# Decoder step on one core: another order of the work in the paged sample attention, and one barrier instead of two at each stage's end

## What is computed

```python
z = rms_norm(h, g) @ w_in
o_a = sparse attention, 8 query heads on 2 K/V heads, top 256 keys of an indexer
o_b = softmax over three dilated windows' denominators, of their outputs
h += (sigmoid(g_A) * (o_a @ w_br_a) + sigmoid(g_B) * (o_b @ w_br_b)) @ w_out
h += memory attention(rms_norm(h)) ; h += swiglu(rms_norm(h)) ; y = rms_norm(h)
```

```python
s = jnp.einsum('bqhgd,bqkhd->bqhgk', qg, k_sel).astype(jnp.float32) * ATTN_SCALE
s = jnp.where(valid[:, :, None, None, :], s, -jnp.inf)
p = jax.nn.softmax(s, axis=-1)
o = jnp.einsum('bqhgk,bqkhd->bqhgd', p.astype(v_sel.dtype), v_sel)
```

```python
wts = jax.nn.softmax(jnp.stack(lses, axis=0), axis=0)
o = jnp.einsum('gbth,gbthd->bthd', wts, jnp.stack(outs, axis=0).astype(jnp.float32))
```

## Time and profile before

| what | value |
|---|---|
| median of three runs | 2143.05 us (2139.27 to 2144.12) |
| profiled execution | 2131.45 us |
| its span | 2129.6 us |
| PE busy | 1971.6 us (93%) |
| DVE busy | 1292.5 us (61%) |
| ACT busy | 709.7 us (33%) |
| POOL busy | 617.9 us (29%) |

### The profile page before, as it was taken

One profiled execution on the slowest core, in us unless ns is written; L12 is line 12 of the kernel. 1 busy time (PEld: TensorE's weight loads), 2 busy tenths in 40 slices (PEclk: granted clock), 3 DMA queues, 4 the chain that ended last, 5 costly groups with the idle time before them and its releaser, 6 DMA issues. The chain is left out here.

```text
span 2129.6 us, 35124 instructions
## 1 busy us (share of the span) xinstructions
PE 1971.6 (93%) x13501; PEld 1815.2 (85%) x13501; DVE 1292.5 (61%) x2478; ACT 709.7 (33%) x1456; POOL 617.9 (29%) x720
## 2 busy tenths in 40 slices
PE   6999899999999896899589989899999999999997
PEld 6878798999997794555379988899999999999997
DVE  5049999999970454543456234786676766643535
ACT  5243222112212572343222135643232332332423
POOL 5786647678980232100200110300000000301000
PEclk9999999999999896999889999899999999999999
DMA  5022232345855726871366102022222222635334
GB/s 178 19 85 76 67 91 78 105 152 176 257 167 159 246 64 170 278 257 60 102 190 177 40 22 80 25 63 81 81 71 86 73 84 81 217 96 166 128 91 137
DMA packets 224858, 254.16 MB, mean 119 GB/s; under 512 B 51684, under 2 KB 206468, under 8 KB 224180
## 3 DMA queue, kind: packets, MB, share of 16 engines
q1 hardware_dynamic: 192292, 170.92, 26.9%
q0 software_dynamic: 9360, 54.37, 7.2%
q10 hardware_dynamic: 23040, 26.63, 3.5%
HBM read 205.18 MB, written 74.00 MB: 131 GB/s over the span
## 5 line engine op out<-in xcount | busy, mean ns | idle before, releaser
L955 PE MATMUL pz<-w_hi,n_hi 128*128 128x384 f32 (+2 forms) x720 | 245.3, 341 | 0.6 <-issue 0.5
L955 PE MATMUL pz<-w_hi,n_lo 128*128 128x384 f32 (+2 forms) x720 | 239.3, 332 | 0.0
L955 PE MATMUL pz<-w_lo,n_hi 128*128 128x384 f32 (+2 forms) x720 | 239.2, 332 | 0.0
L862 DVE MATCH_REPLACE8 sel<-m,sel 128x1024 f32<-128x1024 f32 (+4 forms) x224 | 205.6, 923 | 0.0
L859 DVE MAX8 m<-sel 128x8 f32<-128x1024 f32 (+4 forms) x224 | 197.8, 927 | 0.2
L3618 PE MATMUL p_c<-n_t_hi,blk 128*128 128x264 f32 x1120 | 191.3, 285 | 1.8 <-DVE blk L3335 1.8
L3618 PEld LDWEIGHTS p_c<-n_t_hi,blk 128*128 128x128 f32 x1120 | 159.0, 188 | 2.0 <-issue 2.0
L955 PEld LDWEIGHTS pz<-w_hi,n_hi 128*128 128x128 f32 x720 | 137.6, 191 | 17.0 <-issue 14.9
L3618 PE MATMUL p_c<-mix_hi,blk 128*128 128x264 f32 x816 | 141.1, 285 | 0.0
L955 PEld LDWEIGHTS pz<-w_hi,n_lo 128*128 128x128 f32 x720 | 137.7, 191 | 0.0
L955 PEld LDWEIGHTS pz<-w_lo,n_hi 128*128 128x128 f32 x720 | 137.7, 191 | 0.0
(11 more groups left out here) (490 smaller groups left out, 5194.9 us busy)
## 6 DMA issues: line engine op xcount, KB each, us to landing
w_raw<-in_w_in SPq DMA_DIRECT2D x26, 768.0 KB, 4.6
blk_raw<-in_w_ffn_in SPq DMA_DIRECT2D x72, 256.0 KB, 2.9
relu<-z_qb SPq DMA_DIRECT2D x24, 512.0 KB, 4.9
blk_raw<-in_w_ffn_out SPq DMA_DIRECT2D x58, 192.0 KB, 2.5
z_b<-z ACTq DMA_DIRECT2D x48, 192.0 KB, 1.9
gates<-z ACTq DMA_DIRECT2D x48, 176.0 KB, 3.0
gate<-gates SPq DMA_DIRECT2D x24, 352.0 KB, 3.6
out_new_win_sample<-in_cache_win_kv POOLq DMA_DIRECT2D x8, 1016.0 KB
```

What stands on the lines that cost most here:

```text
L862: dve.match_replace(out=sel[0:r, o:o + n], in_to_replace=m8[0:r, u, :], in_values=sel[0:r, o:o + n], imm_value=PICKED).then_inc(s_rep, 1)
L955: m = pe.matmul(out, tokens(a, k, i), b[:, n % 2, k, 0:w], start=(k == 0 and p == 0), stop=(k == KC - 1 and p == 2))
```

## The change

It has two parts.

**One barrier.** The callback at a stage's end no longer has the second barrier. POOL still clears the semaphores behind the Block's own barrier; the freed numbers are put at the end of the list of free ones, so that the next stage takes others. Seven stages have it.

**Order in `attend_sample_a`.** PE turns the keys of b = 6 right behind those of 5, and lays the bias and the scores of 4 and 5 and the keys of 7 ahead of the first half's turned probabilities, and the scores of 6 and 7 behind them; `values` is split in `turn_probs` and `values`. Row tiles 0 and 1 stand before `values(0)`, tiles 2 to 7 behind `values(1)`. DVE does the first half's differences, shares and weighted sum before it looks at the second half's weights; then `soft(0)` and `soft(1)`, two row tiles, `out(0)`, `out(1)`, six row tiles. ACT's second exponential for the shares moves behind the keys of b = 5; the exponential of a softmax (`exps`) is split from the copies. No operation is added or removed in the stage.

```diff
-    ctx.callback(lambda: (nc.clear_and_free_semaphores(handles), nc.all_engine_barrier()))
+    def retire():
+        nc.clear_and_free_semaphores(handles)
+        nums = [h.num for h in handles]
+        nc.reset_free_semaphores([x for x in nc.free_semaphores if x not in nums] + nums)
+
+    ctx.callback(retire)
...
+                for b in range(6):
+                    keys(b)
+                    if b in (1, 5):
+                        shares(b // 5)
+                keys(6)
+                exps(0)
+                keys(7)
+                weights(0)
+                for i in range(BETWEEN):
+                    rest_high(i)
+                exps(1)
+                weights(1)
+                for i in range(BETWEEN, NT):
...
-                nearest(0)
-                nearest(1)
                 shares(0)
-                shares(1)
                 dve.wait_ge(s_share, 1)
...
+                shares(1)
...
+                soft(0)
+                soft(1)
+                for i in range(BETWEEN):
+                    rest_low(i)
+                out(0)
+                out(1)
+                for i in range(BETWEEN, NT):
...
-                    if i >= BETWEEN:
-                        pe.wait_ge(s_ptev, 3 if i < 2 * BETWEEN else 6)
+                    pe.wait_ge(s_ptev, 3 if i < BETWEEN else 6)
...
-                def values(u):
+                def turn_probs(u):
+                    pe.wait_ge(s_exp, u + 1)
                     for c in range(3):
-                        pe.wait_ge(s_exp, u + 1)
-                        if c == 0:
-                            pe.wait_ge(s_chi, BETWEEN * (u + 1))
-                            pe.wait_ge(s_clo, BETWEEN * (u + 1))
+                        if u and c == 0:
+                            pe.wait_ge(s_chi, BETWEEN)
+                            pe.wait_ge(s_clo, BETWEEN)
...
+                for b in (0, 2, 4):
+                    if b % 4 == 0:
+                        bias_and_new(b // 4)
+                    if b < 4:
+                        for c in range(2):
+                            turn_half(b + 2, c)
+                    for c in range(2):
+                        score_pair(b, c)
+                    for c in range(2):
+                        turn_half(b + 3, c)
+                    if b == 2:
+                        for c in range(2):
+                            turn_half(6, c)
+                turn_probs(0)
+                for c in range(2):
+                    score_pair(6, c)
+                for i in range(BETWEEN):
+                    turn_rows(i)
+                values(0)
+                turn_probs(1)
+                values(1)
+                for i in range(BETWEEN, NT):
```

More of the change, by code:

```diff
@@ L1953, in weights @@
                 def weights(u):
-                    act.wait_ge(s_sm, u + 1)
-                    act.activation(probs[:, 0:NKS], probs[:, 0:NKS], ACT.Exp, scale=-1.0, bias=st[:, u, 0:1],
-                                   accum_out=st[:, u, 1:2]).then_inc(s_exp, 1)
                     for c in range(3):
@@ L1966, in shares, with exps @@
                     act.activation(ex[:, :, x, :], ex[:, :, x, :], ACT.Exp).then_inc(s_ex, 1)
[L1968 to L1976, removed]
+                def exps(u):
+                    act.wait_ge(s_sm, u + 1)
+                    act.activation(probs[:, 0:NKS], probs[:, 0:NKS], ACT.Exp, scale=-1.0, bias=st[:, u, 0:1],
+                                   accum_out=st[:, u, 1:2]).then_inc(s_exp, 1)
+                for b in range(6):
[11 more added lines that the diff above has]
+                for i in range(BETWEEN, NT):
                     rest_high(i)
@@ L2008, in _, with shares @@
                 q.then_inc(s_qexp, 1)
-                def nearest(half):
+                def shares(half):
                     x = slice(HALF * half, HALF * (half + 1))
@@ L2018, in nearest @@
                     t.then_inc(s_diff, 1)
-                def shares(half):
-                    x = slice(HALF * half, HALF * (half + 1))
                     dve.wait_ge(s_ex, half + 1)
@@ L2142, in values @@
                         t.then_inc(s_pt, 1)
+                def values(u):
                     pe.wait_ge(s_ptev, 3 * u + 3)
```

## The result

| what | before | changed |
|---|---|---|
| median of five runs | 2141.34 us (2139.27 to 2144.12) | 2122.64 us (2118.13 to 2130.16) |
| span of the profiled execution | 2129.6 us | 2120.8 us |
| sample attention, release to release | 64.0 us | 50.7 us |

The ratio is 0.9916, with a 95% interval of 0.9898 to 0.9934: between 14 and 22 us less, 18.0 in the middle. The forecast was 19.6 less (2123.5, the measured median is 2122.64). The ratio with its interval is what is used from here on; quotients of the medians differ from it by up to about 0.001. The ratios are of executions at one speed: one execution of the kernel with 26 transposes, at 2419.11 us and a mean granted clock of 0.755, is in none of them.

What follows compares the result with a forecast made beforehand. PE bounds most stages, standing still longest in `attend_sample_a`, where it waited 11.35 us for DVE's late sum. Stage 15.4 plus barriers 4.2 make 19.6 us off the median 2143.05: 2123.5 us, range 2117 to 2131.

Steps and rivals of the forecast that it cites:

- `values(0)`: First half's values on PE in the sample attention: 3.9 us, from 1047.84 to 1051.73 in the earlier trace.
- `values(1)`: Second half's values on PE in the sample attention: 4.0 us, from 1066.46 to 1070.46 in the earlier trace.
- DVE's chain: DVE up to the first softmax in the sample attention: weighted sum alone, 7.4 us instead of 13.45; `soft(0)` done at 1034.65.
- the new wait: PE waits for `s_sm` at the second bias, after turning keys 5 and 6; about 5 us, released by DVE's L2047.
- The bound of 13.45: Upper bound in us on DVE's weighted sum if nothing becomes faster; as a rival, 2129.5 us in total, chance 0.09.
- the block behind the new wait: PE's bias, scores of 4 and 5 and keys 7, within a term of 7.95 us that also held later scores and row tiles.
- a rival on `merge`: PE's clock stays low through 228 more records in `merge`: 30 us lost, 2153.5 us; chance 0.03 slower, 0.04 gain just eaten.
- The narrow cover: Second softmax ready at 1048.3, PE arriving at 1048.85, so the 3.45 us wait at the second turned probabilities goes.
- The tail: Stage's end behind `values(1)`: 5.25 us, with six row tiles instead of four; the two more, 1.25 us, fit in.
- The barriers: Second barrier dropped at the stages' ends: 3.9 us at six between stages plus 0.3 at the very end, together 4.2.
- its own list of signs: Expected in the changed profile: product, sum and wait times, stage 48 us not 63, one release per stage; also signs of error.

Runs made afterwards that it cites:

- the kernel with 26 transposes: Changed kernel plus 26 identity transposes into p_o, in PE's wait ahead of the second bias: stage 46.3 us, median 2117.27 us, ratio 0.9904 to the kernel before.
- the undone order: Changed kernel with both halves' differences and shares again ahead of DVE's weighted sum, and ACT's second exponential back behind the keys of b = 2: stage 60.6 us.

## Why the prediction was right, and where its terms were off

The direction and the mechanism were right: DVE's chain, the new wait and its place. That the median came within 1 us of the forecast is in part luck. The stage's work was shortened by 12.7 us and not by 15.4; the whole came out at 18.0 (14 to 22) against 19.6; and the forecast was taken off a median of three, 2143.05, where the five executions have 2141.34. What lies between the stage and the whole is the barriers' by difference only. Step by step, for the stage's work from its first load to its last DVE operation (63.2 us before; 50.5 measured, 47.8 forecast):

| step | forecast | measured |
|---|---|---|
| first load to `soft(0)` done | 22.15 | 21.75 |
| second bias, scores of 4 and 5, keys 7 | 5.15 | 9.3 |
| turned probabilities, first half | 2.25 | 1.7 |
| scores of 6 and 7, row tiles 0 and 1 | 2.8 | 2.4 |
| `values(0)` | 3.9 | 2.2 |
| wait and turned probabilities, second half | 2.25 | 3.4 |
| `values(1)` | 4.0 | 3.7 |
| tail | 5.25 | 6.0 |

(The forecast had the second and the fourth line as one block of 7.95. Split, the second is 1051.73 to 1056.87, 5.15, and the rest 2.8.)

- **DVE's chain** held to 0.4 us. A product took 419 ns and a sum 1225. The bound of 13.45 was not needed, and the undone order showed that it is what POOL beside it costs. `soft(0)` began 0.17 us ahead of POOL and took 1.22, 0.18 and 1.25 (1.21 and 1.25 in the earlier trace rows); the wait that the Trainium skill (SBUF — State Buffer, Who interferes with whom) allows for a `tensor_scalar` was not seen, and its contention between an operation with two SBUF inputs and GpSimd's was. As the softmax was first here, the better evidence is its start in the middle of POOL's sum; both read their scores from PSUM, so a `tensor_scalar` with its input in SBUF is not tested by any run.
- **The term that was mis-sized is the block behind the new wait**, 9.3 us against 5.15. The prediction took durations from stretches at the full clock, and put the low clock in a rival on `merge`, some 30 us further on. `merge` kept its length (185.5 against 185.2). The low level came in the new wait itself, 3.45 us long, and cost 4.4 us, as the transposes show that took it away, in two profiles of two.
- **`values(0)`** was too long by as much as 1.7 us. Its row in the trace before lay in a window with a clock of 0.52, and the time was taken as if it belonged to the operation. This error and that of the block behind the wait are of one kind, a duration taken without its clock, with opposite signs (4.15 and 1.7 us), so that they cancel in part. `values(1)` was also taken from such a window (0.50) and came out nearly right, 3.7 against 4.0, only because the clock fell there again.
- **The narrow cover** at the second probabilities, thought to hold by half a us, did not: since `values(0)` was faster, PE arrived early and waited 1.35 us.
- **The tail** was 0.7 longer. The six row tiles ran from 1063.17 to 1067.3, and behind them PE still waited 0.56 us for the rows read back from `o_s`. So the tiles fitted, as forecast. From DVE's last `out(1)` operation to the four last transposes, through `o_s`, it took 3.8 us instead of 3.3, and these transposes took 0.63 us at a clock of 0.50 instead of 0.43.
- **The barriers**, 4.2 us forecast. The ratios give 1.1 and 4.9, the stages 1.3 and 0.5 in two places and nothing clear in the longest one. The size can be right, but it isn't shown by a ratio clear of noise. That the release came earlier by the time of one barrier each time was right; that each stage passes it on to its end was not shown for all.

By its own list of signs: four products in 1.43 us (1.5 to 1.7 forecast), POOL 3 us behind the sum, a wait of 3.45 us at L2123 where 5 was forecast, one over 1 us at the turned probabilities where none was. The low granted clock for over 10 us was named as what would prove it wrong for `merge`; it lasted 9.3 us in the sample attention. In `merge` itself it lasted some 10.6 us (1069.3 to 1079.9), so by the letter this sign was there; but the kernel before has nearly the same (1075.9 to 1085.7), and the stage is no longer for it. The stage's work took 50.5 us where the list has 48.

## What to carry to other kernels

When DVE and POOL share a sum, look at whether they run at the same time: here both halves were faster one after the other, and releasing POOL later moved ten of thirteen us without any edit on the engine that bounds. When an operation's duration is taken from a trace to price a new schedule, read the granted clock of its window with it; a PE row at the low level is not the operation's price, and a new wait can cost more than its length: here 3.45 us of it brought 4.4 more. An execution whose untouched first stage scatters by 10 us tells little of a change of 4; the stages' own lengths, over several profiles, tell more.

## What the runs showed of the hardware

- A wait of PE of 3.45 us was followed by 9.3 us at a clock of 0.53; one of 3.01 us by a bias at full speed and 3.3 us of scores at the low level; filled with 26 transposes, so that 0.61 and 0.94 us of it were left, by none; filled with row tiles and 20 transposes, so that 0.83 us was left, again by a bias at full speed and 3.15 us of scores at a mean clock of 0.60. In the first the level fell 2 us after PE stopped, in the second 2 us after it went on. What the chip looks at in between was not measured.
- DVE's 128x256 product of two SBUF tiles takes 419 ns alone and 830 beside POOL's; POOL's takes 604 with no product of DVE's beside it and some 790 with one. A sum of 128x1024 takes 1.22 and 1.52 on DVE, 2.34 and 3.20 on POOL.
- `attend_sparse`, the same instructions in every kernel here, comes in two groups: 199.2 to 200.1 us with a mean clock of 0.92, and 202.3 to 205.2 with 0.89 to 0.90. `attend_mem` does likewise. So a part of the scatter between executions goes with where the clock falls and rises.
